# Third block of a fused three-block model: output and last down projection with tokens on partitions, residual transposed early, normed residual turned back by diagonal matmuls in two token halves

## The chip, the cores and the metric

The kernel runs on one core of a Trainium2 chip. The time is the device time of one execution in microseconds (us). A core has five engines with queues of their own: PE (TensorE, matrix products; its weight loads are listed as PEld), DVE (VectorE), ACT (ScalarE), POOL (GpSimd) and SP (SyncE, which here only starts DMAs). They meet through semaphores. Matmuls write to PSUM, eight banks of 128 partitions by 512 fp32; everything else lies in SBUF.

## What is computed

Three transformer-like blocks run one after the other on the same 512 tokens of 1024 channels, all in fp32. The change touches the third only. There h, the token mixer and its three gated branches give `merged`; then:

```python
y = merged @ w_o                                        # stage "ro" of the kernel
x = x + gt1 * rms_norm_3(y, g_post_mix[l])
h2 = modulate_3(rms_norm_3(x, g_pre_mlp[l]), sh2, sc2)  # norm 10
x = x + gt2 * rms_norm_3(sq_relu_mlp(h2, w_up[l], w_down[l]), g_post_mlp[l])

def rms_norm_3(x, gain=None):
    y = x * lax.rsqrt(jnp.mean(x * x, axis=-1, keepdims=True) + EPS)
    return y * gain if gain is not None else y
def modulate_3(h, shift, scale):
    return h * (1.0 + scale) + shift
def sq_relu_mlp(h, w_up, w_down):                       # stages "upr" and "dnr"
    a = jax.nn.relu(h @ w_up)
    return (a * a) @ w_down
```

`w_o` is 1024x1024, `w_up` 1024x4096, `w_down` 4096x1024. The mean of squares runs over the 1024 channels of a token.

## The kernel before

**Layout.** Activations have channels on the partitions: the residual X is eight tiles of 128 channels by 512 tokens. A projection tile is 128 output channels by 512 tokens in one PSUM bank. `proj_banks` and `mix_banks` are rings of four banks each; a tile takes the next bank in a fixed list of keys and waits until the one four places earlier has been emptied.

**Split products.** In almost all stages each factor is cut into a rounded part (hi, fp32r) and a rest (lo), and a product is three matmuls: hi·hi, hi·lo, lo·hi. SP loads weights in chunks of 128x1024 fp32 (512 KB) into a raw ring of four slots. ACT rounds a chunk into `weight_hi` (`round_chunk`), DVE subtracts to get `weight_lo` (`rest_chunk`), and semaphore `w_split` counts the chunks that are ready. hi and lo are rings of only two slots (`SPLIT_RING = 2`): chunk n+2 is rounded when PE has finished with chunk n. A chunk serves 24 matmuls of 512 columns, whichever layout it is used in.

**Order.** Each engine's program is written out by hand (`tensor_program`, `scalar_program`, `vector_program`, `gpsimd_program`, `sync_program`) and runs strictly in order; no scheduler moves anything.

**The third block's end, before.** `split_loop("ro")` makes the eight output tiles, channels on partitions. ACT copies each to scratch and squares it; when all eight are done, `sum_squares(("ssy", 0))` adds the squares over the channels with eight fp32 matmuls by a matrix of ones, ACT takes the root, DVE the reciprocal of a 128x512 tile (`inverse`), and DVE scales and adds eight tiles to X (`post_norm`). `norm(10)` then squares X (ACT), adds up the squares (DVE, six additions), sums them over the channels (PE, `row_sums`), takes root and reciprocal, spreads the result over the partitions (PE), and DVE and ACT make the hi and lo parts of h2. `first_pair("upr")` runs the first two of the 32 up tiles as these parts come; tile 2 of `upr` and on run in `split_loop`. `split_loop("dnr")` makes the eight down tiles (k over 32 tiles, four chunks each); after the last of them comes the same `post_norm` and then the output is stored from X, one 256 KB DMA per tile. `keep_clock` puts three matmuls of no use at places where PE waits.

Some stages already have the other layout (`rv`, `fv`, `mv`: `split_token_tiles`, L860): there the activation is the stationary operand, 128 tokens are the partitions of the bank, and 512 output channels are its columns.

Of the kernel before, what the change touches and what calls it, by code (L numbers as in the profile page):

```python
# [19 lines left out]
F32 = mybir.dt.float32  # L20
# [6 lines left out]
P = 128  # L27
# [122 lines left out]
for _name, _n in VECTORS:  # L150
# [18 lines left out]
    ("rg", "feat", 4, 8), ("br", "branch", 48, 8), ("ro", "loop", 8, 8), ("upr", "loop", F3T, 8), ("dnr", "loop", 8, F3T),  # L169
# [7 lines left out]
SPLIT_NORMS = (1, 2, 3, 4, 5, 7, 9, 10)  # L177
# [14 lines left out]
def chunks_of(stage):  # L192
    name, kind, tiles, kt = stage
    if kind == "tok":
        return 4 * ((tiles + 3) // 4)
    if kind == "branch":
        return 32
    return tiles * len(pieces(kt))
# [16 lines left out]
def mixing_keys():  # L215
# [35 lines left out]
    k += [("rot_r", t) for t in range(8)]  # L251
    for h in range(5):
        k += [("stat_r", h - 1)] if h >= 1 else []
        k += [("rs", h, j) for j in range(6)] + [("rout", h)] if h < 4 else []
    k += [("dftl", t, c) for t in range(2) for c in range(2)] + [("four", t) for t in range(2)]
    k += [("sgu", t) for t in range(2)]
    k += [("ssy", 0), ("ss", 10), ("bc", 10), ("ssy", 1)]
# [65 lines left out]
class Chip:  # L323


    def __init__(self, nc, ctx, dram):
# [37 lines left out]
        with ExitStack() as mlstm:  # L364
# [26 lines left out]
            "pr_ready", "sgu_ready", "merged", "relu_ready", "mlp_raw", "mlp_hi", "mlp_mid", "y_sq", "y_summed", "out_ready", "out_stored",  # L391
# [121 lines left out]
    def m_square(self, h, k):  # L513
        return self.T(h + 4 * k)

# [97 lines left out]
def sync_program(nc, sp, c):  # L613
# [52 lines left out]
    for k in range(KD):  # L666
        sp.wait_ge(s["out_ready"], k + 1)
        sp.dma_start(d["out"][k * P:(k + 1) * P, :], c.X(k)).then_inc(s["out_stored"], 16)
# [21 lines left out]
def gpsimd_program(nc, pool, c):  # L690
# [48 lines left out]
    pool.dma_start(c.T(47, 6), d["dist"]).then_inc(s["late_tables"], 16)  # L739
    pool.wait_ge(*c.mix.filled(("rs", 3, 5)))  # L740
# [9 lines left out]
def tensor_program(nc, pe, c):  # L750
    s, proj, mix, T, H = c.sem, c.proj, c.mix, c.T, c.H
# [609 lines left out]
    for t in range(9):  # L1361
# [86 lines left out]
    split_loop("ro", lambda k: c.mid_lo[:, (13 + k) * S:(14 + k) * S], lambda k: c.R(16 + k), lambda k: (s["merged_lo"], k + 1))  # L1448
    sum_squares(("ssy", 0), lambda k: proj.emptied(("ro", k)), lambda k: T(SQ0 + k), KD)
    norm(10)  # L1450
    split_loop("upr", lambda k: c.norm_hi(10, k), c.H_lo, None, norm=10)
    split_loop("dnr", c.relu_hi, c.relu_lo, lambda k: (s["mlp_mid"], 28 if k == 0 else k + 1) if k == 0 or k >= 28 else None)
# [1655 lines left out]
```

## Time and profile before

| | us |
|---|---|
| median of 3 runs | 3523.32 |
| lowest and highest of them | 3518.68, 3525.84 |
| profiled execution, first to last instruction (span) | 3516.5 |
| busy in the span: PE / DVE / ACT / POOL | 3369.4 / 2004.1 / 1091.8 / 119.8 |

The spans in a profile are of one execution. Busy times of PE overlap at their ends, so the start-to-start distance of matmuls is the measure of PE's pace, not the duration of one. PEclk is the clock that TensorE was granted as a share of 2.4 GHz; it has two levels, 1.00 and 0.50, and a value in between is a mean over a stretch. A chain of waits follows the execution back from its last instruction; what isn't in it did not set the end.

### The profile page before, as it was taken

The page shows a single profiled execution, that of the slowest core. Times are in us where ns is not written, and L with a number is a line of the kernel's source. Part 1 is how long each engine was busy: PE and PEld are TensorE (multiplying, and loading weights), DVE is VectorE, ACT ScalarE, POOL GpSimd, SP SyncE. Part 2 cuts the span into 40 slices and gives each one's busy share as a digit, 9 for nine tenths or more (in the row PEclk, how much of TensorE's full clock was granted, in tenths as well). Part 3 has the DMA queues.
Part 4 walks back from the last instruction along what each step waited for, and adds up shares of the span by engine and source line. Part 5 has one row for each costly group of instructions (what it writes and reads, how often), then busy time and mean ns, then how long its engine had stood idle before and what let it go on. Part 6 is the DMA issues. An engine that isn't in the chain of part 4 may idle for free. (4 is left out here: it accounts for less than half of the span.)

```text
span 3516.5 us, 38495 instructions
## 1 busy us (share of the span) xinstructions
PE 3369.4 (96%) x13686; PEld 2500.6 (71%) x13686; DVE 2004.1 (57%) x2790; ACT 1091.8 (31%) x1448; POOL 119.8 (3%) x214
## 2 busy tenths in 40 slices
PE   6999999999899999989999999999999999979997
PEld 3446788887678887667888844688887657758886
DVE  6675766435568855465665289666635533355423
ACT  2223422225432223353333200533332432232221
POOL 1000010000000000000000040000000000000000
PEclk9999999999999999999999999999999999989999
DMA  7222355542135542212323211132333112212232
GB/s 284 80 65 82 116 191 192 170 132 66 42 119 192 191 130 86 77 36 78 101 95 96 90 54 43 60 102 95 96 95 123 58 66 96 96 54 96 96 97 71
DMA packets 100420, 361.12 MB, mean 103 GB/s; under 512 B 11152, under 2 KB 11168, under 8 KB 100064
## 3 DMA queue, kind: packets, MB, share of 16 engines
q1 hardware_dynamic: 79088, 280.34, 24.5%
q0 software_dynamic: 20080, 75.27, 6.5%
q10 hardware_dynamic: 1152, 4.19, 0.3%
q8 instruction: 61, 1.00, 0.1%
q14 instruction: 39, 0.32, 0.0%
HBM read 357.66 MB, written 2.10 MB: 102 GB/s over the span
## 5 line engine op out<-in xcount | busy, mean ns | idle before, releaser
L2103 DVE TENSOR_TENSOR weight_lo<-weight_ring,weight_hi 128x1024 fp32r<-128x1024 f32 (+1 forms) x462 | 557.5, 1207 | 955.5 <-ACT weight_hi L1471 949.7
L1471 ACT ACTIVATE weight_hi<-weight_ring 128x1024 fp32r<-128x1024 f32 (+1 forms) x462 | 482.9, 1045 | 1629.4 <-PE proj_banks L824 1123.4
L824 PE MATMUL proj_banks<-h_lo,weight_hi 128*128 128x512 f32 x1704 | 664.3, 390 | 0.0
L824 PE MATMUL proj_banks<-h_hi,weight_hi 128*128 128x512 f32 x1344 | 524.0, 390 | 4.0 <-DVE weight_lo L2103 4.0
L824 PE MATMUL proj_banks<-h_hi,weight_lo 128*128 128x512 f32 x1344 | 523.6, 390 | 0.0
L824 PEld LDWEIGHTS proj_banks<-h_lo,weight_hi 128*128 128x128 f32 x1704 | 320.6, 188 | 66.3
L824 PE MATMUL proj_banks<-mid_lo,weight_hi 128*128 128x512 f32 x768 | 299.2, 390 | 0.0
L824 PEld LDWEIGHTS proj_banks<-h_hi,weight_hi 128*128 128x128 f32 x1344 | 252.6, 188 | 58.2 <-issue 5.6
L824 PEld LDWEIGHTS proj_banks<-h_hi,weight_lo 128*128 128x128 f32 x1344 | 252.7, 188 | 52.4
L824 PE MATMUL proj_banks<-mid_hi,weight_lo 128*128 128x512 f32 x704 | 273.9, 389 | 0.0
L824 PE MATMUL proj_banks<-mid_hi,weight_hi 128*128 128x512 f32 x704 | 273.9, 389 | 0.0
L770 PE MATMUL proj_banks<-h_tiles,weight_ring 128*128 128x512 f32 x528 | 233.4, 600 | 3.5 <-ACT h_tiles L1471 3.5
L824 PE MATMUL proj_banks<-relu_hi,weight_hi 128*128 128x512 f32 x522 | 197.4, 393 | 7.6 <-DVE weight_lo L2103 7.6
L770 PEld LDWEIGHTS proj_banks<-h_tiles,weight_ring 128*128 128x128 f32 x528 | 101.8, 193 | 131.8 <-issue 130.0
L2111 DVE SCALAR_TENSOR_TENSOR scratch<-proj_banks,vectors,scratch 128x511 f32<-128x511 f32 (+3 forms) x208 | 155.2, 746 | 26.3 <-ACT scratch L1471 12.7
L824 PEld LDWEIGHTS proj_banks<-mid_lo,weight_hi 128*128 128x128 f32 x768 | 144.2, 188 | 29.9 <-issue 0.2
L2103 DVE TENSOR_TENSOR scratch<-scratch 128x512 f32<-128x512 f32 (+6 forms) x224 | 158.3, 707 | 12.4 <-ACT scratch L1471 2.5
L824 PE MATMUL proj_banks<-relu_hi,weight_lo 128*128 128x512 f32 x410 | 160.8, 392 | 0.0
L824 PEld LDWEIGHTS proj_banks<-mid_hi,weight_lo 128*128 128x128 f32 x704 | 132.2, 188 | 27.6
L824 PEld LDWEIGHTS proj_banks<-mid_hi,weight_hi 128*128 128x128 f32 x704 | 132.2, 188 | 27.5
L2111 DVE SCALAR_TENSOR_TENSOR scratch<-scratch,vectors 128x512 f32<-128x512 f32 x190 | 142.9, 752 | 6.7
L1471 ACT ACTIVATE scratch<-proj_banks 128x512 f32<-128x512 f32 (+1 forms) x178 | 100.6, 572 | 141.4 <-PE proj_banks L770 68.5
(370 smaller groups left out, 4883.0 us busy)
## 6 DMA issues: line engine op xcount, KB each, us to landing
weight_ring<-in_w_up SPq DMA_DIRECT2D x176, 512.0 KB, 3.5
ada_ring<-in_ada POOLq DMA_DIRECT2D x96, 512.0 KB, 3.9
weight_ring<-in_w_dn SPq DMA_DIRECT2D x64, 512.0 KB, 3.6
weight_ring<-in_w_br SPq DMA_DIRECT2D x32, 512.0 KB, 3.6
weight_ring<-in_w_upr SPq DMA_DIRECT2D x32, 512.0 KB, 3.5
weight_ring<-in_w_dnr SPq DMA_DIRECT2D x32, 512.0 KB, 3.4
weight_ring<-in_w_dn SPq DMA_DIRECT2D x32, 384.0 KB, 3.1
cond<-in_ada POOLq DMA_DIRECT2D x20, 512.0 KB, 4.6
```

The source lines that it names most:

```text
L770: last = mm(bank[:, 0:n], c.slot(chunk)[:, i * P:(i + 1) * P], rhs(k), start=k == 0, stop=k == sum(per) - 1)
L824: last = mm(proj.banks[:, u % RING, :], stationary(split0 + n)[:, w], moving(k), start=k + m == 0, stop=k == kt - 1 and m == 2)
L1471: return nc.scalar.activation(out, in_, func, **kw)
L2103: return v.tensor_tensor(out, a, b, op)
L2111: return v.scalar_tensor_tensor(out=out, in0=a, scalar=x, in1=b, op0=op0, op1=op1)
```

## The change

**Stages.** `ro` and `dnr` become token stages with 2 x 4 tiles: in part 0 four token tiles by channels 0 to 511, in part 1 channels 512 to 1023. The new `token_stage` goes through the chunks (4 per part for `ro`, 16 for `dnr`), each for all four token tiles; the last two chunks of part 1 are taken token by token, so that token tile t is finished while t+1 runs. It waits for both of these chunks before it starts them. For `ro` they have places of their own (`held`), as have the first two chunks of `upr` (`first_up`); for `dnr` they lie in the two slots of the ring.

**Norms.** The mean of squares of a token is now a sum along the row of a partition: ACT's Square with `accum_out`, a 128x1 root, and DVE's 128x1 reciprocal. DVE multiplies each bank by a gain row (`gained`), then scales it by the token's column and adds the residual (`new_residual`, and the last lines of the program, which write the output tiles).

**Residual.** While `rk` and `rq` run, PE transposes X in 32 squares (key `xt`), and ACT copies it back; from there X(k) holds, for channel tile k, tokens on partitions. **Gain rows**: POOL makes 16 diagonal 128x128 tiles of the gains (`grow_diag`), PE spreads them with four fp32 matmuls by ones (key `grow`), and ACT copies them out.

**h2.** `norm(10)` and `first_pair("upr")` go. For each half of the tokens (`half_turned`) PE multiplies X's squares by a diagonal of the token scales, which transposes and normalises at once, into bank key `ht`; ACT makes hi with gain and shift from that bank, DVE raw and lo. `half_pair` runs the first two up tiles on the 256 columns of that half. The `keep_clock` matmuls of this place are gone too.

The core of the diff:

```diff
+    for t in range(8):
+        k += [("rot_r", t), ("xt", t)]
...
+    pool.wait_ge(s["x_ready"], KD)
+    pool.wait_ge(*c.mix.filled(("rot_r", 7)))
+    for n in range(2):
+        for k in range(KD):
+            nc.gpsimd.tensor_scalar(c.gain_row(n, k // 4)[:, k % 4 * P:(k % 4 + 1) * P], c.square("ident"), c.g(7 + n, k), None, ALU.mult) \
+                .then_inc(s["grow_diag"], 1)
...
+            bank = open_bank(mix, ("xt", t - 1))
+            pe.wait_ge(s["x_ready"], t)
+            for j in range(NB):
+                last = nc.tensor.transpose(bank[:, j * P:(j + 1) * P], X(t - 1)[:, j * P:(j + 1) * P], c.square("ident"))
+            last.then_inc(mix.full_sem, 1)
...
+    for n in range(4):
+        bank = open_bank(mix, ("grow", n))
+        pe.wait_ge(s["grow_diag"], 4 * (n + 1))
+        mm(bank, c.square("ones"), c.gain_row(n // 2, n % 2), start=True, stop=True).then_inc(mix.full_sem, 1)
...
+        for part in range(2):
+            for q in range(chunks if part == 0 else chunks - 2):
+                n = chunks * part + q
+                pe.wait_ge(s["w_split"], first + n + 1)
+                for t in range(NB):
+                    last = products(n, part, q, t)
...
+        pe.wait_ge(s["w_split"], first + 2 * chunks)
+        for t in range(NB):
+            for q in range(chunks - 2, chunks):
+                last = products(chunks + q, 1, q, t, held and held(q - chunks + 2))
+            last.then_inc(proj.full_sem, 1)
...
+    def half_turned(half):
+        pe.wait_ge(s["h10_diag"], 2 * half + 2)
+        for b in range(4):
+            bank = open_bank(mix, ("ht", half, b))
+            for k in range(2 * b, 2 * b + 2):
+                for t in range(2 * half, 2 * half + 2):
+                    at = k % 2 * 256 + t % 2 * P
+                    last = mm(bank[:, at:at + P], X(k)[:, t * P:(t + 1) * P], c.token_scale(t), start=True, stop=True)
+            last.then_inc(mix.full_sem, 1)
+    def half_pair(half):
+        cols = slice(256 * half, 256 * (half + 1))
+        for k in range(KD):
+            pe.wait_ge(s["h10_hi"], KD * half + k + 1)
...
+                for n, part in enumerate(c.first_up(t)):
+                    mm(bank[:, cols], part[:, w], hi10(k)[:, cols], start=k + n == 0, stop=False, skip_group_check=True)
+        for k in range(KD):
+            pe.wait_ge(s["h10_lo"], KD * half + k + 1)
...
+    def root_residual(t):
+        for p in range(2):
+            act.wait_ge(s["x_new"], 2 * t + p + 1)
+            st.link(f(T(32).rearrange("p (k f) -> p k f", k=4), c.x_token(t, p), ACT.Square, accum_out=c.x_stat(p, t)))
...
+    for n in range(SPLIT_RING, 17):
+        round_chunk("dnr", n)
+    for t in range(NB):
+        square_token("dnr", 0, t, H(4))
+    first_half_stat()
+    for n in range(17, F3T):
+        round_chunk("dnr", n)
+    for t in range(NB):
+        root_token("dnr", t, H(4))
...
+        for p in range(2):
+            out = columns4(c.late_tile(4 * p + t))
+            st.done(stt(out, out, c.y_scale(t), c.x_token(t, p), ALU.mult, ALU.add), s["out_ready"])
```

PE's program between the last `ro` products and tile 2 of `upr`. `late_rounded` is the hi part of h2, `x_tiles` X, `others` and `squares` constants. Before:

```order
L890 MATMUL mix_banks<-scratch,squares 128x512 x8
L902 MATMUL mix_banks<-squares 128x256 x3
L927 MATMUL mix_banks<-scratch,others 4x128 x8
L902 MATMUL mix_banks<-squares 128x256 x3
L936 MATMUL mix_banks<-scratch,others 128x128 x4
L902 MATMUL proj_banks<-squares 128x256 x3
L785 MATMUL proj_banks<-late_rounded,weight_hi 128x512
L786 MATMUL proj_banks<-late_rounded,weight_lo 128x512
```

After (L1554 is `half_turned`, L1568 and L1572 are `half_pair`; the first row is the last product of `ro`):

```order
L1523 MATMUL proj_banks<-relu_hi,mid_lo 128x512
L1554 MATMUL mix_banks<-scratch,x_tiles 128x128 x16
L1568 MATMUL proj_banks<-late_rounded,relu_lo 128x256 x32
L1572 MATMUL proj_banks<-h_lo,relu_lo 128x256 x16
L1554 MATMUL mix_banks<-scratch,x_tiles 128x128 x16
L1568 MATMUL proj_banks<-late_rounded,relu_lo 128x256 x32
L1572 MATMUL proj_banks<-h_lo,relu_lo 128x256 x16
L875 MATMUL proj_banks<-late_rounded,weight_hi 128x512
```

All matmuls over sums of squares are gone; 32 squares of 128x128 and 96 products of half the width stand in their place.

DVE's program at the same place, before, from the last residual tile to the lo parts of h2:

```order
L2111 SCALAR_TENSOR_TENSOR scratch<-scratch,gain 128x512
L2103 TENSOR_TENSOR x_tiles<-x_tiles,scratch 128x512
L2103 TENSOR_TENSOR scratch<-scratch 128x512 x6
L2103 TENSOR_TENSOR weight_lo<-weight_ring,weight_hi 128x1024
L2151 RECIPROCAL scratch<-scratch 4x128
L2103 TENSOR_TENSOR weight_lo<-weight_ring,weight_hi 128x1024
L2111 SCALAR_TENSOR_TENSOR h_tiles<-x_tiles,gain,mix_banks 128x512 x8
L2111 SCALAR_TENSOR_TENSOR h_lo<-h_tiles,mod,late_rounded 128x512 x8
```

After, from `gained` of token tile 2 into the first half's split (the 128x128 row is the diagonal of token scales):

```order
L2285 TENSOR_TENSOR scratch<-proj_banks,ada_ring 128x512
L3131 RECIPROCAL small<-small 128x1
L2293 SCALAR_TENSOR_TENSOR x_tiles<-scratch,small,x_tiles 128x4x128 x2
L3131 RECIPROCAL small<-small 128x1
L2289 TENSOR_SCALAR scratch<-squares,small 128x128
L2285 TENSOR_TENSOR scratch<-proj_banks,ada_ring 128x512
L3131 RECIPROCAL small<-small 128x1
L2293 SCALAR_TENSOR_TENSOR x_tiles<-scratch,small,x_tiles 128x4x128 x2
L2290 TENSOR_SCALAR scratch<-mix_banks,gain,mod 128x256 x2
L2285 TENSOR_TENSOR h_lo<-scratch,late_rounded 128x256 x2
```

The work per token tile is now short and repeats four times, and the diagonal of tile 1 stands behind the residual of tile 2.

## Rows read from the trace of the kernel before

**Rows 1.** Head of the page.

```profile
span 3516.5 us, 38495 instructions
```

**Rows 2.** Chain that ended last, in order of time: start us, us, what.

```profile
3094.82 12.01 PE proj_banks L824 x53
3106.84 6.88 PE mix_banks L890 x16
...
3115.80 3.36 DVE scratch L2137
...
3130.57 0.70 DVE x_tiles L2103
...
3135.67 3.57 PE mix_banks L927 x16
...
3142.06 0.76 DVE h_tiles L2111
...
3154.77 0.51 PE proj_banks L790
...
3157.84 337.56 PE proj_banks L824 x1488
3495.43 0.60 ACT cond L1471
...
3498.62 3.36 DVE scratch L2137
...
3513.38 0.69 DVE x_tiles L2103
```

**Rows 3.** Timeline of SP at the end: start us, us, what.

```profile
3503.51 10.93 SPq L668 DMA_DIRECT2D out<-x_tiles  x8
```

**Rows 4.** ACT instructions grouped by form: count, busy us, mean ns, idle before.

```profile
L1471 ACT ACTIVATE scratch<-proj_banks 128x512 f32<-128x512 f32 x165 | 95.8, 586 | 124.8 <-PE proj_banks L770 61.3 <-PE proj_banks L824 33.5 <-PE proj_banks L879 19.6
L1471 ACT ACTIVATE scratch<-mix_banks,small 128x256 f32<-128x256 f32 x8 | 3.4, 470 | 0.1
L1471 ACT ACTIVATION_READ_ACCUMULATOR scratch<-scratch,small 128x1 f32 x16 | 3.0, 187 | 0.0
L1471 ACT ACTIVATE small<-small,others 128x8 f32<-128x8 f32 x1 | 0.3, 301 | 0.0
```

**Rows 5.** DVE instructions grouped by form, same columns.

```profile
L2396 DVE RECIPROCAL small<-small 128x1 f32<-128x1 f32 x16 | 2.6, 164 | 0.7 <-DVE relu_lo L2103 0.2
L2103 DVE TENSOR_TENSOR scratch<-scratch,mix_banks 128x256 f32<-128x256 f32 x4 | 1.7, 420 | 0.1
```

**Rows 6.** Timeline of PE in the first block: start us, us, what, count.

```profile
367.56 0.60 PE L1130 MATMUL mix_banks<-squares,scratch 128*128 128x128 f32 x4
367.99 1.06 PE L1137 MATMUL mix_banks<-scratch 128*128 128x128 f32 x8
```

**Rows 7.** Stretches with busy times of the engines, then PEclk, DMA share, GB/s.

```profile
367.50:369.00 1.50, 1.50 (x13) 1.30 (x11) 0.90 (x2) 1.22 (x3) 0.00 (x0) 1.00 0.13 52
...
389.00:394.00 5.00, 5.00 (x22) 4.13 (x23) 4.89 (x7) 0.77 (x2) 1.06 (x2) 1.00 0.66 208
968.20:973.00 4.80, 4.80 (x14) 3.80 (x15) 2.33 (x3) 0.76 (x2) 0.00 (x0) 0.64 0.69 208
```

**Rows 8.** Timeline of PE: two waits for a split chunk, idle time in brackets.

```profile
389.00 0.47 PE L824 MATMUL proj_banks<-relu_hi,weight_hi 128*128 128x512 f32 x1 [1.89 <-DVE weight_lo L2103]
...
968.19 0.72 PE L824 MATMUL proj_banks<-relu_hi,weight_hi 128*128 128x512 f32 x2 [1.89 <-DVE weight_lo L2103]
```

**Rows 9.** Timeline of PE in stage `rv`, already a token stage.

```profile
2731.41 0.39 PE L860 MATMUL proj_banks<-weight_hi,mid_hi 128*128 128x512 f32 x1
2731.64 0.39 PE L860 MATMUL proj_banks<-weight_hi,h_lo 128*128 128x512 f32 x1
```

**Rows 10.** POOL instructions grouped by form, columns as in rows 4.

```profile
L734 POOL TENSOR_SCALAR scratch<-squares,vectors 128x128 f32<-128x128 f32 x66 | 42.9, 665 | 413.6 <-PE proj_banks L824 413.6
```

**Rows 11.** Timeline of PE at the start of the branch stage.

```profile
2875.00 0.79 PE L1438 MATMUL proj_banks<-mid_hi,weight_hi 128*128 128x512 f32 x1 [4.03 <-DVE cond L2103]
```

More of the change, by code:

```diff
@@ L1456 @@
+    for half in range(2):
+        half_turned(half)
+        half_pair(half)
+    split_loop("upr", hi10, c.H_lo, None, started=True)
+    token_stage("dnr", c.relu_hi, c.relu_lo, None, lambda k: (s["mlp_mid"], 28 if k == 0 else k + 1) if k == 0 or k >= 28 else None)
 ATT = (16, 20, 21, 9)
@@ L1976, in scalar_program @@
             head_stat(mix, ("rout", h), T(57), c.late_tile(0))
+    for n in range(4):
+        copy_out(mix, ("grow", n), c.gain_row(n // 2, n % 2))
     for t in range(2):
@@ new lines, in round_to, with round_half @@
+    def round_to(name, n, hi):
+        chunk = c.first_chunk[name] + n
+        act.wait_ge(*c.chunk_landed(chunk))
+        st_round(f(hi, c.slot(chunk), ACT.Copy))
+    def round_half(half):
+        use, layer, part, ready = MODULATED[10]
+        cols = slice(256 * half, 256 * (half + 1))
+        if half == 0:
+            act.wait_ge(s["mod_ready"], ready)
+        for k in range(KD):
+            act.wait_ge(*mix.filled(("ht", half, k // 2)))
+            bank = mix.bank(("ht", half, k // 2))[:, k % 2 * 256:(k % 2 + 1) * 256]
+            st.done(f(c.norm_hi(10, k)[:, cols], bank, ACT.Identity, scale=c.g(use, k), bias=c.m(layer, part, k)), s["h10_hi"])
@@ new lines, in scalar_program @@
+    set_table(ACT.Sqrt)
+    for n in range(SPLIT_RING, 5):
+        round_chunk("ro", n)
+    for t in range(NB):
+        square_token("ro", 0, t, T(32))
+    first_half_stat()
+    round_chunk("ro", 5)
+    for n in range(2):
+        round_to("ro", 6 + n, c.held(n)[0])
+    for n in range(2):
+        round_to("upr", n, c.first_up(n)[0])
+    for t in range(NB):
+        root_token("ro", t, T(32))
+        if 1 <= t < 3:
+            root_residual(t - 1)
+    round_half(0)
+    for t in range(2, 4):
+        root_residual(t)
@@ L2019, in scalar_program @@
+    for n in range(SPLIT_RING):
+        round_chunk("upr", SPLIT_RING + n)
+    round_half(1)
     u0 = proj.number[("upr", 0)]
@@ L2933, in vector_program, with rest_to @@
     branch_tiles(3, last=True)
-    def post_norm(stage, r, y, at, gain, sem):
-        if stage == "ro":
-            for n in range(SPLIT_RING, KD):
-                rest_chunk(stage, n)
-        inverse(("ssy", r), T(RSTD))
-        for k in range(KD):
-            st.link(stt(y(at + k), y(at + k), c.g(gain, k), T(RSTD), ALU.mult, ALU.mult))
-            st.done(tt(X(k), X(k), y(at + k), ALU.add), sem)
-    post_norm("ro", 0, T, 27, 7, s["x_ready"])
-    norm(10)
+    def rest_to(name, n, parts):
+        dve.wait_ge(s["w_rounded"], c.first_split[name] + n + 1)
+        hi, lo = parts
+        tt(lo, c.slot(c.first_chunk[name] + n), hi.bitcast(F32), ALU.subtract).then_inc(s["w_split"], 1)
@@ new lines, in gained, with inverse_column, columns4, new_residual @@
+    def gained(stage, p, t, out, row, done):
+        dve.wait_ge(s["y_sq"], done + NB * p + t + 1)
+        st.last(tt(out, proj.bank((stage, NB * p + t)), row, ALU.mult), proj.emptied((stage, NB * p + t)))
+    def inverse_column(col, sem, n):
+        dve.wait_ge(sem, n)
+        st.link(v.reciprocal(col, col))
+    def columns4(ap):
+        return ap.rearrange("p (k f) -> p k f", k=4)
+    def new_residual(t):
+        for p in range(2):
+            st.done(stt(c.x_token(t, p), columns4(c.ro_out(t, p)), c.y_scale(t), c.x_token(t, p), ALU.mult, ALU.add), s["x_new"])
@@ L2947, in vector_program @@
+    split_half(0)
+    for t in range(2, 4):
+        token_scales(t)
+    for n in range(SPLIT_RING):
+        rest_chunk("upr", SPLIT_RING + n)
+    split_half(1)
     u0 = proj.number[("upr", 0)]
```

201 lines of the change are left out of this document (142 added, 59 removed).

## The prediction, made before the result was known

> **What bounds the kernel now.** I read four views. The page gives the span, 3516.5 us [rows 1], and PE's busy share of 96%, so most of the time is PE's own pace and a change can win only where PE stands still. The chain of waits in order of time shows where that is in the third block [rows 2]. After the last `ro` product, at 3106.84, PE first does the eight sums over the channels (6.88 us), then DVE's reciprocal of a whole tile (3.36) and sixteen residual operations run until 3131.3, then six additions, then PE sums and spreads from 3135.67, and DVE works out h2 from 3142.06; only at 3157.84 does tile 2 of `upr` start. Between lie 51.0 us, of which the first two up tiles need 48 products of 0.227, 10.9 us; some 40 us are a seam. The second standstill is the end: the last down product ends about 3495.3, copy, square, sum, root, the 3.36 us reciprocal and sixteen DVE operations take it to 3514.1, and the last store ends the span at 3516.5, so 21.2 us [rows 1 to 3]. Third, rows for single forms give the prices. Fourth, the rows of stage `rv` show that a product with tokens on partitions costs the same as any other: starts 0.23 us apart [rows 9]. So the 192 products of `ro` and the 768 of `dnr` keep their time and only what stands around them moves. My sum is made on the span; the median of the runs is 6.8 us above it (3523.3 against 3516.5), and I add that at the end.
>
> **The seam after `ro`, now 51.0 us.** Call the end of the last `ro` product 0. In the last section a token tile takes 12 products, 2.7 us, so the tiles fill at -8.2, -5.4, -2.7 and 0. Per tile ACT squares the bank (0.59 for a PSUM read of that size, and between 0 and 0.19 for the accumulator read, depending on how far it overlaps; I take 0.1) and takes a 128x1 root (0.30), 1.06 with the gaps [rows 4]. DVE multiplies by the gain row (0.70), inverts a column (0.16) and does two residual operations of 0.76, together 2.5 with the gaps [rows 2, 5]. ACT also squares the new residual twice and takes two small steps, 2.2 us, in between. Played through in each engine's order, ACT is late by a little: it ends tile 1's residual statistic at +1.3, DVE makes the diagonal by +1.8, and PE starts `half_turned(0)` at +1.9. PE has 16 fp32 matmuls of 128 columns there. One is two instructions, and eight such instructions took 1.06 us, starts about 0.115 apart [rows 6], so 3.8 us. DVE ends tile 3's residual at +4.6 and then splits half 0: eight operations from PSUM and eight subtractions on 256 columns at 0.42 and a gap of 0.03 [rows 5], 7.2 us, to +11.8. ACT's eight roundings at 0.47 [rows 4] and PE's 48 half-width products are done sooner than that, so **DVE is the bound here**; PE ends half 0 at +12.2. DVE then needs 1.0 for the diagonals of tiles 2 and 3, PE turns half 1 from 12.9 to 16.7, and DVE meanwhile splits two weight chunks (2.5) and then half 1 (7.2), ending at 22.5. PE follows with its last lo products at +22.9. For PE's clock I add 0.4: PE stands 1.9 us before `half_turned(0)`, and after equal waits it was granted 1.00 in one row and 0.64 in another [rows 7, 8]; most of a slow spell here hides behind DVE. So 23.3 instead of 51.0: **-27.7**.
>
> The half-width products aren't in the trace. Their bounds: 0.115 us apart, as the fp32 instructions of rows 6 (each streams its 128 columns twice, as many as 256 once), and 0.227, as full-width ones [rows 9]. I take 0.12 since the streamed amount and the weight load are those of rows 6. At that price they are covered by DVE; at 0.227 they aren't (first rival).
>
> **The end, now 21.2 us.** After the last product: ACT's wake-up and square 0.8, DVE's gain product 0.75 and column 0.2 (the root, ready at +1.1, hides behind it), two scaled additions 1.55, so the last store starts at +3.4; before, it started at 3514.1 and the span ended 2.4 later, so +5.8. The three earlier token tiles need 2.5 us of DVE each against PE's 2.7, so none queues up. **-15.4**.
>
> **The refill before the last two `dnr` chunks.** PE waits for both chunks, but the slot of chunk 31 is free only when chunk 29 is done, and ACT's rounding and DVE's subtraction come after. The nearest rows are the waits of 1.89 us in which a pair of tiles ends together [rows 8]; there the first tile of the pair, whose end frees the slot, ends 0.68 before the second. Here nothing runs in that time: 1.89 + 0.68, and PE's overlap of one product with the next lost, 2.8 in all. Waits of 1.86 to 1.94 us of this kind occur six times in the trace, and in four the clock was about 0.6 for the next 4 to 5 us; in such a stretch 14 products ran in 4.8 us instead of 21 [rows 7], 1.6 lost. I take it: **+4.4**, between 2.8 and 4.4. Nothing is queued behind that wait except ACT's last squares. `ro` has no such wait, since chunks 6 and 7 have places of their own and are split some 9 us before use. At the boundary of parts ACT rounds chunk 17 after four squares; that is ready at +3.4 of the 5.4 us that chunk 16 takes.
>
> **Transposes of X.** 32 in eight groups of four in stages `rk` and `rq`, where PE runs without a pause. Four took 0.43 us at full clock, from 367.56 to 367.99 [rows 6]. Bounds: 8 x 0.43 = 3.4, and twice that at the lower clock, 6.9. I take 0.5 each, nearest to the row and a little for the change to the products after it: **+4.0**. ACT's eight copies (0.60) fall into idle time of 4 to 5 us per tile, and so do not cost; if that cover went, 4.8.
>
> **Gain rows.** Four fp32 matmuls by ones at 6.88/8 = 0.86 [rows 2] are 3.4, and ACT's first copy delays the next bank by 0.2. They stand ahead of the Fourier and gating products, whose last link DVE is waited for at the start of the branch stage [rows 11], so the whole chain slides: **+3.6**. POOL's 16 diagonals at 0.665 are 10.6 us [rows 10] on an engine with nothing else to do, started some 100 us before they are used; they cost nothing, and would only if the start came less than 11 us ahead.
>
> **Sum.** -27.7 - 15.4 + 4.4 + 4.0 + 3.6 = -31.1: a span of 3485.4 and a median of about **3492 us**, 0.9% less.
>
> **Rivals.** (1) *Short matmuls don't pay in the seam.* If a 256-column product costs what a 512-column one does, or PE runs the seam at 1.2 GHz because it waits so often there, PE becomes the bound: per half 32 x 0.215 + 48 x 0.22 = 17.5, two halves and the first 1.9 make 36.9 instead of 23.3, so 13.6 more: 3506. For it: waits of under 2 us did lower the clock [rows 7, 8]. Against: the fp32 rows of rows 6 show twice the rate. (2) *Strided reads of the token view.* The residual of a token is four pieces of 128, 2 KB apart. If DVE took 1.5 us for such an operation instead of 0.76, it would need 4.0 us a tile and fall behind PE's 2.7, by some 5 us at either seam: 3502. Against: nothing in the rows shows a penalty for pieces; no row has this very view. (3) *The transposes cool the clock, and the kernel is slower.* If the granted clock fell to 1.2 GHz for the eight `rk`/`rq` tiles because transposes interrupt them, each tile's 24 products would take 5.4 us more, 8 x 5.4 = 43.5, and the kernel would end 12 above, at 3536; it turns from gain to loss once six of the eight tiles run so. Against: in the stretch with four transposes and eight fp32 instructions the granted clock was 1.00 [rows 7]. The Trainium skill, "TensorE: Matmul & The Clock Gate", section "Part 4: PE-mode transpose", says that the full clock doesn't engage for transposes. By that rule the time would be nearer to this rival's; the trace disagrees with it for groups as short as these, with its 1.00.
>
> **How the numbers follow.** Forecast 0.70, spread over 3484 to 3498 (clock terms of 2 us, transposes 3.4 to 6.9, and the median's own 3.6 either way); rival 1 0.17, rival 2 0.08, rival 3 0.02, something unseen 0.03, mostly a smaller gain. The range takes in the forecast, rival 2 and half of rival 1: 3484 to 3505. A measurement of this kernel can tell about 0.2%, 7 us, from no change. All cases but rival 3 and a part of the unseen are faster by more: faster 0.95, same 0.03, slower 0.02.
>
> **What the changed profile would show.** From the last `ro` product to tile 2 of `upr` about 23 us with DVE busy almost throughout; half-width products 0.12 apart when they don't wait; one wait of PE of 2 to 3 us for a split chunk, 11 us before the last down product; four transposes in 0.5 us; four grow matmuls in 3.5; from the last product to the end of the span about 6 us. Wrong if the turned matmuls start 0.2 us apart, if the seam takes over 30 us, if DVE operations on the token view take clearly over 0.8, or if `ro` or `dnr` show waits at other chunks.

## The result, and the profile of the changed kernel

Four executions of the changed kernel took 3494.78 us in the median (3490.96 to 3498.58), four of the kernel before beside them 3521.0 (3518.15 to 3525.84). The ratio is 0.9925, with a 95% interval of 0.9911 to 0.9938: 0.75% faster, where 0.9% was forecast (3492 us). The profiled execution took 3490.96 with a span of 3489.3.

So the span fell by 27.2 us, from 3516.5 [rows 1], and not by 31.1. Chain that ended last, in order of time: start us, us, what; the rows that answer to [rows 2].

```profile
3070.67 38.11 PE proj_banks L1523 x168
...
3115.29 0.70 ACT scratch L1599 x2
...
3117.00 0.76 DVE x_tiles L2293
...
3118.58 0.55 DVE scratch L2290
...
3139.21 0.97 PE proj_banks L1572 x4
3140.18 164.84 PE proj_banks L875 x720
3305.02 163.21 PE proj_banks L1523 x720
3468.25 1.06 ACT weight_hi L1599
...
3469.34 1.24 DVE weight_lo L2285
...
3470.62 10.09 PE proj_banks L1523 x36
...
3481.08 0.70 ACT h_tiles L1599 x2
```

L875 is the product line of `split_loop`, L1523 that of `token_stage`. The sums over the channels and both reciprocals of whole tiles are gone; ACT's roots and DVE's short operations stand in their place, and a refill before the last down products is new. As PE's timeline has it (start, us, what, count, idle time in brackets):

```profile
3470.62 0.50 PE L1523 MATMUL proj_banks<-weight_hi,h_rounded 128*128 128x512 f32 x1 [2.41 <-DVE weight_lo L2285]
```

Timeline of PE from the last `ro` product to the second product of tile 2 (start, us, what, count, idle time in brackets):

```profile
3113.82 0.39 PE L1523 MATMUL proj_banks<-relu_hi,mid_lo 128*128 128x512 f32 x1
3115.90 3.84 PE L1554 MATMUL mix_banks<-scratch,x_tiles 128*128 128x128 f32 x32 [1.70 <-DVE scratch L2289]
3119.50 4.08 PE L1568 MATMUL proj_banks<-late_rounded,relu_lo 128*128 128x256 f32 x32
...
3126.94 0.96 PE L1572 MATMUL proj_banks<-h_lo,relu_lo 128*128 128x256 f32 x4 [1.24 <-DVE h_lo L2285]
3128.44 3.84 PE L1554 MATMUL mix_banks<-scratch,x_tiles 128*128 128x128 f32 x32 [0.54 <-DVE scratch L2289]
3132.04 4.08 PE L1568 MATMUL proj_banks<-late_rounded,relu_lo 128*128 128x256 f32 x32
3135.95 2.02 PE L1572 MATMUL proj_banks<-h_lo,relu_lo 128*128 128x256 f32 x12
3139.21 0.97 PE L1572 MATMUL proj_banks<-h_lo,relu_lo 128*128 128x256 f32 x4 [1.24 <-DVE h_lo L2285]
3140.01 0.57 PE L875 MATMUL proj_banks<-late_rounded,weight_hi 128*128 128x512 f32 x1
3140.38 0.63 PE L875 MATMUL proj_banks<-h_lo,weight_hi 128*128 128x512 f32 x1
```

Every wait of PE in it is for DVE. The seam, from the end of the last `ro` product to the start of tile 2, lasts from 3114.2 (3115.90 less the wait of 1.70) to 3140.01, 25.8 us. DVE's forms in the third block's end (count, busy us, mean ns, idle before):

```profile
L2290 DVE TENSOR_SCALAR scratch<-mix_banks,gain,mod 128x256 f32<-128x256 f32 x16 | 8.7, 543 | 0.6
L2285 DVE TENSOR_TENSOR h_lo<-scratch,late_rounded 128x256 fp32r<-128x256 f32 x16 | 6.8, 425 | 1.5 <-DVE scratch L2290 1.3
L2293 DVE SCALAR_TENSOR_TENSOR x_tiles<-scratch,small,x_tiles 128x512 f32<-128x512 f32 x8 | 6.0, 752 | 0.3
```

And the stretches that answer to [rows 7] (busy times of the engines, then PEclk, DMA share, GB/s): the start of the branch stage, the seam, the first products of tile 2, and those behind the refill.

```profile
2882.40:2887.20 4.80, 4.78 (x11) 3.84 (x12) 0.00 (x0) 0.00 (x0) 0.00 (x0) 0.50 0.00 0
3116.00:3140.00 24.00, 20.78 (x160) 19.17 (x161) 21.11 (x42) 15.40 (x31) 0.00 (x0) 1.00 0.14 45
3140.00:3143.40 3.40, 3.40 (x11) 2.66 (x10) 2.44 (x4) 1.08 (x2) 0.00 (x0) 0.51 0.00 0
3470.60:3475.00 4.40, 4.38 (x12) 3.48 (x13) 0.00 (x0) 0.00 (x0) 0.00 (x0) 0.61 0.00 0
```

The new operations upstream, in order: the transposes of one tile of `rk`, the gain rows, and POOL's diagonals (the last two rows are groups by form).

```profile
2682.07 0.60 PE L1423 MATMUL mix_banks<-squares,x_tiles 128*128 128x128 f32 x4
2682.42 0.47 PE L897 MATMUL proj_banks<-mid_hi,weight_hi 128*128 128x512 f32 x1
...
2855.10 1.88 PE L1459 MATMUL mix_banks<-ada_ring,squares 128*128 128x512 f32 x4
...
2859.08 13.97 PE L1465 MATMUL mix_banks<-scratch 128*128 128x512 f32 x32 [0.39 <-ACT ada_ring L1599]
...
L789 POOL TENSOR_SCALAR ada_ring<-squares,gain 128x128 f32<-128x128 f32 x8 | 8.8, 1115 | 82.2 <-PE mix_banks L992 82.2
L789 POOL TENSOR_SCALAR squares<-squares,gain 128x128 f32<-128x128 f32 x8 | 5.4, 693 | 0.0
```

The account against the trace of before, on the span: the last `ro` product ends 7.4 us later (3114.2 against 3106.84), the seam is 25.2 shorter (25.8 against 51.0), from tile 2 to the end of `dnr` it takes 5.9 more (343.4 against 337.5), and from there to the end of the span 15.3 less (5.9 against 21.2). Together -27.2.

### The profile page after: what moved, and what is told of

Its sections match the earlier page's. It is cut to its first block and busy times, and to the rows that moved or that the text cites. A ratio compares the mean times of both kernels' runs of the same rounds, so it can differ in the third digit from the quotient of the medians.

```text
span 3489.3 us, 38628 instructions
## 1 busy us (share of the span) xinstructions
PE 3370.3 (97%) x13776; PEld 2507.8 (72%) x13776; DVE 1995.6 (57%) x2807; ACT 1098.5 (31%) x1491; POOL 134.1 (4%) x230
## 5 line engine op out<-in xcount | busy, mean ns | idle before, releaser
L875 PE MATMUL proj_banks<-h_lo,weight_hi 128*128 128x512 f32 x1704 | 664.9, 390 | 0.0
L875 PE MATMUL proj_banks<-h_hi,weight_hi 128*128 128x512 f32 x1344 | 523.9, 390 | 4.0 <-DVE weight_lo L2285 4.0
L875 PE MATMUL proj_banks<-h_hi,weight_lo 128*128 128x512 f32 x1344 | 523.5, 389 | 0.0
L875 PEld LDWEIGHTS proj_banks<-h_lo,weight_hi 128*128 128x128 f32 x1704 | 321.0, 188 | 66.6
L875 PEld LDWEIGHTS proj_banks<-h_hi,weight_hi 128*128 128x128 f32 x1344 | 252.6, 188 | 57.9 <-issue 5.7
L875 PEld LDWEIGHTS proj_banks<-h_hi,weight_lo 128*128 128x128 f32 x1344 | 252.7, 188 | 52.7
L875 PE MATMUL proj_banks<-mid_hi,weight_hi 128*128 128x512 f32 x704 | 273.9, 389 | 0.0
L875 PE MATMUL proj_banks<-mid_lo,weight_hi 128*128 128x512 f32 x704 | 273.9, 389 | 0.0
L875 PE MATMUL proj_banks<-mid_hi,weight_lo 128*128 128x512 f32 x704 | 273.9, 389 | 0.0
L2293 DVE SCALAR_TENSOR_TENSOR scratch<-proj_banks,vectors,scratch 128x511 f32<-128x511 f32 (+3 forms) x208 | 155.2, 746 | 26.3 <-ACT scratch L1599 12.7
L875 PEld LDWEIGHTS proj_banks<-mid_lo,weight_hi 128*128 128x128 f32 x704 | 132.2, 188 | 27.5
L875 PEld LDWEIGHTS proj_banks<-mid_hi,weight_hi 128*128 128x128 f32 x704 | 132.2, 188 | 27.4
L875 PEld LDWEIGHTS proj_banks<-mid_hi,weight_lo 128*128 128x128 f32 x704 | 132.2, 188 | 27.4
L1599 ACT ACTIVATE scratch<-proj_banks,vectors 128x512 f32<-128x512 f32 x112 | 83.9, 749 | 159.9 <-PE proj_banks L821 159.9
```

Of the source, the lines that this page charges most:

```text
L875: last = mm(proj.banks[:, u % RING, :], stationary(split0 + n)[:, w], moving(k), start=k + m == 0, stop=k == kt - 1 and m == 2)
L1599: return nc.scalar.activation(out, in_, func, **kw)
L2293: return v.scalar_tensor_tensor(out=out, in0=a, scalar=x, in1=b, op0=op0, op1=op1)
```

## The experiments

Each is one edit of the changed kernel. The changed kernel's own executions lie up to 7.6 us apart, and the trace shows differences of that kind in a part that no edit touches (last section). So three places are read apart, from the one execution of each kernel that was profiled: where the last `ro` product ends, where tile 2 of `upr` starts, and the span.

| kernel | last `ro` product | seam | tile 2 to the end | ratio to before, 95% |
|---|---|---|---|---|
| changed kernel | 3114.2 | 25.8 | 349.3 | 0.9925 (0.9911 to 0.9938) |
| dnr_last_held | 3119.8 | 25.8 | 344.8 | 0.9907 (0.9886 to 0.9928) |
| ro_last_in_ring | 3118.3 | 26.3 | 347.6 | 0.9932 (0.9915 to 0.9948) |
| seam_short_doubled | 3113.9 | 28.1 | 347.6 | 0.992 (0.99 to 0.9941) |
| seam_rest_from_neg | 3113.2 | 23.5 | 347.7 | 0.9901 (0.988 to 0.9922) |
| seam_pool_rests | 3113.1 | 30.8 | 347.6 | 0.9921 (0.9901 to 0.994) |
| seam_pool_early | 3114.8 | 30.2 | 347.7 | 0.9926 (0.991 to 0.9943) |
| seam_filled_wait | 3113.3 | 26.7 | 347.7 | 0.9922 (0.9907 to 0.9937) |
| seam_filled_before | 3119.7 | 25.8 | 346.0 | 0.9902 (0.9886 to 0.9919) |
| transposes_in_wait | 3109.5 | 26.7 | 346.1 | 0.9903 (0.9887 to 0.9918) |
| three_edits | 3119.1 | 23.5 | 343.3 | 0.9908 (0.9893 to 0.9922) |
| four_edits | 3113.5 | 23.5 | 343.3 | 0.9882 (0.9866 to 0.9898) |

The ratio is of whole executions, of which each kernel had four or five. Only the last one's is clear of the changed kernel's; what the others show is read from the trace.

**The refill, taken away.**

```diff
-    token_stage("dnr", c.relu_hi, c.relu_lo, None, ...)
+    token_stage("dnr", c.relu_hi, c.relu_lo, c.last_held, ...)   # chunk 31 in h_rounded, tiles 4 to 7
-    for n in range(17, F3T):
+    for n in range(17, F3T - 1):
         round_chunk("dnr", n)
+    round_to("dnr", F3T - 1, c.last_held(1)[0])
```

> Chunk 31 of the last down projection gets a place of its own (four tiles that are free by then), is rounded right behind chunk 30 and split early; the throw-away output of the squares goes to an unused PSUM bank. Theory (the refill wait costs its own length and the half-speed stretch behind it): the wait of 2.41 us before the last 24 products goes, and with it the PEclk of 0.61 over the next 4.4 us (12 products in 4.4 instead of 2.7, so 1.7 us): the span is 4.1 us shorter than the changed kernel's 3489.3, so 3485.2. Rival (the low clock is not due to the wait and appears there or a little later anyway): 2.4 us shorter, 3486.9, with PEclk still near 0.6 in those 5 us. The rest of the profile is as it was.

Measured: no wait, and PEclk 1.00 up to the last product:

```profile
3470.00:3484.00 14.00, 14.00 (x64) 11.58 (x63) 7.65 (x13) 3.42 (x10) 0.00 (x0) 1.00 0.19 69
```

From tile 2 to the end 344.8 instead of 349.3, though tile 2 itself began at the half clock as before. That is 4.5 us less. The wait makes up 2.6 of it (over it two products start 2.79 apart, 3467.83 and 3470.62, instead of 0.23) and its slow stretch 1.7. The whole span was longer (3490.5), because the last `ro` product ended 5.6 later in this execution; read by the span alone the edit would seem worthless.

**The refill, put in at the other place.** In `ro`, where the change gives the last chunks places of their own, they go back into the ring.

```diff
-    for n in range(2):
-        round_to("ro", 6 + n, c.held(n)[0])
+    for n in range(2):
+        round_chunk("ro", 6 + n)
```

> The last two chunks of the output projection lose their own places and go through the two ring slots, as those of the down projection do in the changed kernel. Theory (the refill wait is worth its 2.41 us wherever it stands, and up to 1.6 more where a slow stretch follows it): PE waits 2.3 to 2.5 us for a split chunk 13.3 us before the seam; the seam itself keeps its 25.8 us; the span 2.4 to 4.0 us longer than 3489.3 in a like execution, 3491.7 to 3493.3. Rival (part of it is given back: the seam starts with ACT and DVE less behind): under 2 us.

```profile
3105.51 0.61 PE L1523 MATMUL proj_banks<-weight_hi,mid_lo 128*128 128x512 f32 x1 [2.40 <-DVE weight_lo L2285]
```

The wait is there at its full length, the products behind it are 0.43 apart until 3109, and the last `ro` product ends 4.1 us later. Upstream this execution had the clock pattern of the changed kernel's (last section), so the 4.1 is the wait and its slow stretch. The seam didn't give it back (26.3). 1.7 came back behind it, since tile 2 ran at full clock this time; the span rose by 2.9. What the forecast said of the covered `ro` is so measured: those places are worth 4 us.

**The short products, doubled.**

```diff
                 for n, part in enumerate(c.first_up(t)):
-                    mm(bank[:, cols], part[:, w], hi10(k)[:, cols], ...)
+                    for twice in range(2):
+                        mm(bank[:, cols], part[:, w], hi10(k)[:, cols], ...)
```

> Each of the 64 half-width products with a hi activation is issued twice, so the values of the first two up tiles are not the reference's. Theory (a 256-column product costs 0.12 us, and DVE is the bound, so that part of them is hidden): PE gets 3.9 us more work in each half. In half 0 the products end at about 3127.4 instead of 3123.5, the lo products then follow without waits until 3129.3, 0.9 later than DVE had released half 1; half 1 has 3.8 + 7.8 + 2.0 = 13.6 us of PE work, to 3142.9 instead of 3140.0: the span 2.9 us longer. Rival (PE is the bound): 7.8 longer. Rival (the busier PE also keeps its clock at tile 2, where it was granted 0.51 for 3.4 us): 2.9 - 1.7, 1.2 longer, with PEclk 1.00 behind the seam.

Timeline of PE:

```profile
3119.18 7.92 PE L1569 MATMUL proj_banks<-late_rounded,relu_lo 128*128 128x256 f32 x64
3126.94 2.08 PE L1573 MATMUL proj_banks<-h_lo,relu_lo 128*128 128x256 f32 x16
```

64 products in 7.76, 0.12 apart: that price holds. 7.8 us of added work lengthened the seam by 2.3, so 5.5 of it lay beside DVE; PE had that much room. And tile 2 ran at full clock: in sum only 0.6.

**The lo part of h2, made in another way.** DVE takes the shift minus hi first, which needs only SBUF, and then adds bank times gain.

```diff
-                ins = ts(T(8 + k)[:, 0:256], bank, c.g(use, k), ALU.mult, c.m(layer, part, k), ALU.add)
+                ins = ts(T(8 + k)[:, 0:256], hi, -1.0, ALU.mult, c.m(layer, part, k), ALU.add)
...
-                st.done(tt(c.H_lo(k)[:, cols], T(8 + k)[:, 0:256], hi, ALU.subtract), s["h10_lo"])
+                st.done(stt(c.H_lo(k)[:, cols], bank, c.g(use, k), T(8 + k)[:, 0:256], ALU.mult, ALU.add), s["h10_lo"])
```

> The lo part of h2 is formed differently on DVE: first shift minus hi, from SBUF with one per-partition scalar and a constant, then bank x gain + that, straight into h_lo. In the changed kernel a pair was 0.55 (from PSUM with two scalars) + 0.44. Theory (an operation reading PSUM costs 0.55 and one on SBUF alone about 0.3, and DVE is the bound): 0.85 for a pair with no more gap, 2.2 us per bank become 1.7 to 1.9, so split_half(0) ends 1.2 to 2 us earlier, and since everything behind it starts from there, split_half(1) too: seam 2.4 to 4 us shorter, but ACT's roundings of half 1 and PE's turning may eat a part; 2 us less as my value. Rival (the time per operation does not depend on the source, 0.55 each): no gain, or 0.1 us more per pair, 1.6 us longer.

Timeline of DVE:

```profile
3117.59 0.74 DVE L2290 TENSOR_SCALAR scratch<-late_rounded,mod 128x256 f32<-128x256 f32 x2
3118.37 1.01 DVE L2293 SCALAR_TENSOR_TENSOR h_lo<-mix_banks,gain,scratch 128x256 fp32r<-128x256 f32 x2
```

0.37 and 0.50 in place of 0.55 and 0.44, and a bank now takes 1.94 instead of 2.20. Eight banks make 2.1; the seam is 2.3 shorter. This shows directly that DVE's split operations set the seam's length. Tile 2 at full clock adds 1.7.

**Weight subtractions on POOL.** They leave DVE, first in their old place, then earlier.

```diff
+    for n in range(SPLIT_RING, 2 * SPLIT_RING):          # POOL
+        nc.gpsimd.tensor_tensor(c.lo(split), c.slot(chunk), c.hi(split).bitcast(F32), ALU.subtract)
...
-    for n in range(SPLIT_RING):                          # DVE
-        rest_chunk("upr", SPLIT_RING + n)
```

> The two weight subtractions (chunks 2 and 3 of the last up projection, 1.2 us each on DVE) that stand between the two halves of the seam go from DVE to POOL, which is idle. Theory (DVE is the bound of the seam): split_half(1) starts 2.4 us earlier, unless ACT's hi parts are then the last: in the changed kernel these began at 3129.64 and need 4.75, so they would allow DVE a start near 3130.7 against 3130.84, and moving DVE's work gains nothing at the start of half 1 because PE turned half 1 only from 3128.44 on, waiting for DVE's diagonals of tokens 2 and 3. So theory in full: gain about 0.1 to 0.5 us in the seam (25.8 us), not 2.4. Rival (DVE's sum of work alone sets the seam): 2.4 us less, 23.4. POOL takes 1.5 to 4 us for each of them; if its access disturbs DVE's, DVE operations at its side get longer and the seam too.

Neither theory held; the seam grew by 5.0. What happened is what the expectation names last, a disturbance of DVE. Timelines of POOL and DVE:

```profile
3126.30 4.65 POOL L798 TENSOR_TENSOR weight_lo<-weight_ring,weight_hi 128x1024 fp32r<-128x1024 f32 x2 [292.89 <-ACT weight_hi L1603]
...
3126.39 2.34 DVE L2293 TENSOR_SCALAR scratch<-squares,small 128x128 f32<-128x128 f32 x1
3128.77 0.16 DVE L3135 RECIPROCAL small<-small 128x1 f32<-128x1 f32 x1
3128.97 2.06 DVE L2293 TENSOR_SCALAR scratch<-squares,small 128x128 f32<-128x128 f32 x1
```

The two diagonals take 0.29 elsewhere. Here each ends within 0.1 us of the end of one of POOL's operations. PE waited 4.37 us for them, and had a PEclk of 0.61 afterwards.

> POOL does the two weight subtractions as in the earlier POOL kernel, but ACT rounds the two chunks right behind the first half's roundings, so POOL works while DVE splits half 0. Theory (a POOL operation that reads SBUF shuts out, to its end, the DVE operations that need two SBUF inputs or run as a 128x128 tensor_scalar from SBUF; one reading PSUM and SBUF or PSUM alone goes on): POOL runs 2 x 2.3 us from about 3123; the 128x256 TENSOR_SCALAR from PSUM keeps its 0.55, and one to three h_lo subtractions (0.44) take up to 2.3 us; half 0 ends 2 to 3.5 us later, and since the 2.4 us of weight subtractions are gone from DVE, the seam is 25 to 27 us, about as long as 25.8. Rival (only TENSOR_SCALAR from SBUF is shut out, as the two diagonals were): the h_lo subtractions keep 0.44 and the diagonals of tokens 2 and 3, which DVE reaches after 3127.4, are undisturbed; the seam is limited by ACT's residual statistics, which now come 2 us later: 25 to 26. The durations of the h_lo rows tell the two apart, not the seam.

```profile
3123.73 4.88 POOL L798 TENSOR_TENSOR weight_lo<-weight_ring,weight_hi 128x1024 fp32r<-128x1024 f32 x2 [288.50 <-ACT weight_hi L1603]
...
3123.59 1.13 DVE L2294 TENSOR_SCALAR scratch<-mix_banks,gain,mod 128x256 f32<-128x256 f32 x2
3124.86 4.04 DVE L2289 TENSOR_TENSOR h_lo<-scratch,late_rounded 128x256 fp32r<-128x256 f32 x2
```

The operation that reads PSUM keeps its 0.56 beside POOL; two subtractions with both inputs in SBUF take 4.04 instead of 0.88. The first theory held on the rows. Its seam (25 to 27) didn't: it was 30.2, since half 1 was turned 3.1 later and its turned matmuls took 6.27 instead of 3.84; they followed four waits of PE, of 1.29, 2.00, 1.23 and 0.24, and PEclk was 0.59 from 3132.2 to 3138.4. The Trainium skill, "SBUF — State Buffer", section "Who interferes with whom", says that a DVE instruction with two SBUF inputs contends with a GpSimd instruction that reads SBUF, and that the second to issue blocks until the first finishes. These rows agree: POOL's two operations end at 3128.61 and the two subtractions at 3128.90. That sentence doesn't cover the diagonals of seam_pool_rests, which have one tile and one column from SBUF; that they were held up as well stands on their own rows. Contention of this kind would also fit the 1.115 us of the first eight diagonals of POOL upstream, beside DVE's subtractions, against 0.693 of the others; that this is their cause was not tried.

**PE's clock behind the seam.** Five matmuls of no use at the last wait:

```diff
+            if half == 1 and k == 6:
+                for _ in range(5):
+                    mm(mix.bank(("ht", 1, 0))[:, 0:P], c.square("ones"), c.sq_const[:, 0:P], start=True, stop=True)
```

> Five 128-column fp32 matmuls of no use (ten instructions, 1.2 us) are put before the lo products of channel tile 6 of the second half, where PE waits 1.24 us for DVE at the end of the seam. Theory (the PEclk of 0.51 over the first 3.4 us of tile 2 comes from that wait): the wait shrinks to about 0.1, the seam stays 25.8 us, and tile 2 starts at PEclk 1.00: the stretch from tile 2 to the end is 347.6 us instead of 349.3. Rival (it comes from the waits of the seam before that, 1.70 and 0.54, or from the half-width products as such): no change, 349.3.

The edit put them behind the wait, not before it. So PE stood still 1.24 us as ever, the seam grew by 0.9, and tile 2 ran at full clock all the same: 347.7. Put before the wait:

> As the earlier kernel with a filled wait, whose five matmuls of no use started only after the wait of 1.24 us; here they stand before it, so that PE works through it (ten instructions of 0.12 us). Theory (the slow stretch at tile 2 follows PE's standing still): wait for the lo part at most 0.1 us, seam 25.8 to 25.9 us, tile 2 at PEclk 1.00, 347.6 us from tile 2 to the end against 349.3. Rival (the clock at tile 2 depends on where the seam lies in time as much as on the wait: the filled kernel before kept its wait and tile 2 still ran at 1.00): the same result here can't tell them apart, but a PEclk of 0.5 at tile 2 would speak for the rival alone.

```profile
3143.36 1.28 PE L1573 MATMUL mix_banks<-squares 128*128 128x128 f32 x10
3144.76 0.96 PE L1576 MATMUL proj_banks<-h_lo,relu_lo 128*128 128x256 f32 x4
3145.56 0.39 PE L875 MATMUL proj_banks<-late_rounded,weight_hi 128*128 128x512 f32 x1
```

The wait is filled, the seam keeps its 25.8, tile 2 runs at 1.00. But in the same execution the wait of 2.41 us before the last `dnr` products was there and no slow stretch followed it either (346.0). The slow stretches stand behind waits, but not behind every one: after 2.40 or 2.41 us PEclk was 0.61 in the changed kernel and 1.00 here and in the next one. The theory that the 1.24 us wait alone brings the low clock at tile 2 doesn't hold: the first of these two kernels kept the wait, and so does the next one, with no matmul of no use behind it (3135.41, the first products of tile 2 then 0.23 to 0.24 apart). What decides it was not found.

**The transposes, moved into a wait.**

```diff
-            for j in range(NB):                                          # in the rk/rq tiles
-                last = nc.tensor.transpose(bank[:, j * P:(j + 1) * P], X(t - 1)...)
...
+    for t in range(KD):                                                  # before the branch stage
+        bank = open_bank(mix, ("xt", t))
+        for j in range(NB):
+            last = nc.tensor.transpose(bank[:, j * P:(j + 1) * P], X(t)...)
```

> The 32 transposes of X leave the rk/rq tiles and go into PE's wait of 4.03 us at the start of the branch stage, with their eight ACT copies. Theory (a group of four costs 0.43 us between two tiles; the half-speed products behind the wait come from PE having stood still): the rk/rq tiles are 6.35 us apart again instead of 6.78, 8 x 0.43 = 3.4 us less; at the branch stage two groups fill two free banks, the others wait for banks that DVE and ACT empty (0.6 us a copy), so PE is done about 1.1 us after the moment at which DVE releases it now; and the 12 products that ran at half speed there (0.43 apart, 2.4 us lost) run at full speed. Span 3489.3 - 3.4 + 1.1 - 2.4 = 3484.6. Rival (transposes don't count for the clock, so the stretch behind them is slow as before): 3487.0, with PEclk 0.50 for the first four us of the branch stage. Rival (transposes cost much more there): over 3489.

```profile
2874.95 1.53 PE L1483 MATMUL mix_banks<-squares,x_tiles 128*128 128x128 f32 x12
2877.93 2.40 PE L1483 MATMUL mix_banks<-squares,x_tiles 128*128 128x128 f32 x20 [1.45 <-DVE cond L2287]
2880.09 0.47 PE L1501 MATMUL proj_banks<-mid_hi,weight_hi 128*128 128x512 f32 x1
...
2878.00:2882.20 4.20, 4.20 (x29) 3.87 (x30) 0.60 (x1) 3.37 (x6) 0.00 (x0) 1.00 0.00 0
```

The branch stage starts 2.3 us earlier (2880.09 against 2882.42), as 3.4 - 1.1 says, and its first products run at full clock: the last `ro` product ends 4.7 earlier, all of it as expected. The four executions took 3483.49 to 3484.3. Twenty transposes stood directly ahead of the products, and PEclk was 1.00 in both, as in the stretch of [rows 7]. The Trainium skill, "TensorE: Matmul & The Clock Gate", section "Part 4: PE-mode transpose", has it that the full clock doesn't engage for transposes; this trace disagrees in so far as the clock stayed at 1.00 through them; it was 1.00 before them too (2868 to 2875), and no run shows whether it would rise while only transposes run.

**Versions put together.** `three_edits` is the held chunk 31, the new lo part, and the subtraction of chunk 3 moved behind the second half. `four_edits` also moves one wait that was in both kernels:

```diff
-    pe.wait_ge(s["sgu_ready"], 2)
     with pe.Fori(0, 4) as i:
...
+            if g == 5:
+                pe.wait_ge(s["sgu_ready"], 2)
```

> Together: chunk 31 of the last projection in a place of its own, the lo part of h2 from shift minus hi, and the weight subtraction of chunk 3 of the last up projection behind the second half instead of before it. Theory: from the span of the changed kernel, 3489.3, go 4.4 (measured for the first), 2.3 + 1.7 (for the second, the clock of tile 2 among it) and 0.4 to 0.9 for the third, because DVE, which releases PE, has 1.2 less to do before the end of half 1 but PE's own work in half 1 is 9.4 us and started only at 3126.4: a seam of 22.6 to 23.1 us and a span of 3480.2 in an execution that is like the changed kernel's profiled one up to the seam; ratio to before 0.989. Rival (chunk 3 then comes late for tile 3): PE waits at tile 3 for up to 1 us and the clock falls there.

> As the one with three edits, and PE waits for the gating product only at the tile that reads it (the sixth of the branch stage), not before the stage. Theory: the wait of 4.03 us at its start shrinks to what ACT's last Fourier copy still takes (0.5 to 1 us after the gating products were issued, so about 0), the 12 half-speed products behind it (2.4 us) run at full speed: 4.0 + 2.4 = 6.4 less, a span near 3473.8, ratio 0.987. Rival (the next wait takes its place, for a weight chunk or the first gating operands): 2 to 4 us less.

From the last `ro` product to the end three_edits takes 366.8 us against 375.1, 8.3 less, where 8.8 to 9.3 were expected. The third edit gave nothing: the seam is 23.5 with it and without. With 1.2 us less to do, DVE only waits 1.07 for ACT's first hi parts of half 1; the order diagonal, PE, ACT, DVE sets the start of that half. It did so, by a hair, in the changed kernel already: there DVE was through with the weight chunks at 3130.78, and ACT's second hi part came at 3130.81. So taking the weight subtractions away could start half 1 only 0.03 us earlier. The executions of three_edits ran from 3481.84 to 3489.83. In four_edits the wait at the branch stage is gone; the last `ro` product ends 5.6 earlier than in three_edits (6.4 expected). The expectation took the 2.4 that the half clock cost in the changed kernel; in three_edits PEclk behind the wait was 0.64 from 2888.1 to 2892.9, with 14 products instead of 21, which is 1.6. The median is 3480.62 (3471.3 to 3481.97), 1.2% below before: the best version.

## Why the prediction was right, and where not

**The seam, 27.7 forecast, 25.2 measured.** Its order of events was right to a tenth or two at first: PE began `half_turned(0)` at +1.7 (+1.9), DVE the split at +4.4 (+4.6). The step that failed is the price "at 0.42 and a gap of 0.03": the nearest row [rows 5] has both operands as tensors and no per-partition scalars. The TENSOR_SCALAR from PSUM took 0.55, and a gap of 0.16 stands before each pair of subtractions, so 2.20 us a bank instead of 1.8. That is 1.6 a half and 3.2 in all; the 0.4 for the clock that wasn't needed and 0.3 of smaller items bring the difference to 2.5. That DVE is the bound was right (doubled products: 5.5 of 7.8 us hidden; a cheaper pair: 2.3 less). ACT's rounding of 256 columns was priced too low as well, 0.47 against 0.57; eight took 4.75 us, which stayed beside DVE's work but for the first two of half 1.

**The end, 15.4 forecast, 15.3 measured.** 5.9 us from the last product: ACT's wake-up and square to 3484.2, then DVE 2.46 from 3484.38 to 3486.84, and the span ends 2.4 later as before. DVE had finished the tile before only at 3484.34, 0.1 after ACT's square, so "none queues up" is not quite true.

**The refill, 4.4 forecast.** The forecast had 2.8 for the wait with the lost overlap and 1.6 for the clock. The wait was 2.41, 2.6 with the overlap, and the slow stretch behind it 1.7. The held chunk gave 4.5 back. The size was right, though the clock part doesn't come each time: it did in seven of the nine profiled kernels that have this wait.

**From tile 2 to the end of `dnr` 5.9 in all.** The 1.5 beyond the forecast's 4.4 is a place that it did not name: the first eight intervals between products of tile 2 were 0.37 to 0.43 instead of 0.23. Of the twelve profiled kernels only this one and dnr_last_held show it, so it belongs to the execution more than to the change. It had put its clock term at the start of the seam, where the clock was 1.00.

**The transposes, +4.0.** Tiles are 6.78 us apart instead of 6.35, 8 x 0.43 = 3.4, the lower bound. ACT's copies were hidden as said.

**The gain rows, +3.6.** 3.98 from 2855.10 to 2859.08: the ACT wait behind them was 0.39, not 0.2, and the overlap with the next matmul was lost on top. POOL took 14.2 us for its 16 diagonals, not 10.6, hidden all the same.

**The rivals.** Short products that don't pay: false, 0.12 apart, and PE had PEclk 1.00 from 3116 to 3140. Strided reads: false, 0.752 for the token view, where 0.76 was taken. Transposes that cool the clock: false, 6.78 a tile, and PEclk 1.00 behind 20 of them.

**The step from span to median.** The forecast added 6.8 us, the median less the profiled span of before. Of these, 1.6 lay around the span of the profiled execution (3518.15 against 3516.5), and the other 5.2 are what this execution lay below the median. After the change the same distance is 5.5 (3494.78 against 3489.3). So the forecast was 3.9 too hopeful on the span (3485.4), 1.3 of that was made good by this step, and the median was missed by 2.6. That part of the agreement is luck.

## What to carry to other kernels

When sums over partitions are turned into sums along rows, look next at the engine that does the elementwise split, and price each of its forms from a row with the same source (PSUM or SBUF) and the same kind of operands. A double-buffered chunk that is needed together with its neighbour costs its whole refill; one spare place for the last chunk is enough. Work that is moved to POOL and reads SBUF must not run beside DVE operations that take two inputs from SBUF, or beside a TENSOR_SCALAR from SBUF, if someone waits for them; both were held up here until POOL was through.

## What the runs showed of the hardware

A TENSOR_SCALAR from PSUM with two per-partition scalars on 128x256 takes 0.55 us, from SBUF with one 0.37. POOL's 128x1024 subtraction takes 2.3 us and stops a DVE TENSOR_SCALAR of 128x128 from SBUF (2.34 instead of 0.29) and two-input subtractions (4.04 for two instead of 0.88), not the TENSOR_SCALAR from PSUM.

The same code upstream gets the half clock in different places from one profiled execution to the next. Two stretches in the first quarter of the program, first of three_edits, then of the changed kernel; no edit reaches there:

```profile
808.00:816.00 8.00, 7.13 (x21) 4.92 (x21) 3.00 (x4) 4.13 (x7) 0.00 (x0) 0.79 0.20 66
860.00:866.00 6.00, 6.00 (x16) 4.03 (x15) 0.13 (x1) 4.50 (x9) 0.00 (x0) 0.59 0.25 87
```

```profile
808.00:816.00 8.00, 6.58 (x23) 3.79 (x23) 4.03 (x5) 4.38 (x7) 0.00 (x0) 1.00 0.13 41
860.00:866.00 6.00, 6.00 (x29) 5.00 (x28) 0.00 (x0) 5.88 (x10) 0.00 (x0) 1.00 0.27 87
```

In 860 to 866 that is 16 matmuls against 29. Of the kernels with no edit ahead of the seam, those with this pattern (three_edits, dnr_last_held, seam_filled_before) end their last `ro` product at 3119.1 to 3119.8, those with the changed kernel's pattern at 3113.1 to 3114.8: 5 to 6 us. four_edits had the slow pattern too. The changed kernel's own executions lie on two levels 7.5 apart (3491.0 and 3498.5); that these patterns are the reason is likely, but only one of its executions has a trace. What picks one pattern stays open.
